# Two layers of a hybrid decoder on one core: meetings with fewer waits for stores, a tile ahead of its meeting, and one sum fewer per selection pass

## What is computed

```python
def split_in(h): ...
    (cb, cc, ch, cg, sq, sk, sv, sg, dq, dk, dv, dg, iq, ik, iw) = split_in(h)
def stick_breaking(q, k, v, q_pos, k_pos):
    z = jnp.einsum('bqhd,bkhd->bhqk', q, k).astype(jnp.float32) * HEAD_DIM ** -0.5
    after = lax.cumsum(log_keep, axis=3, reverse=True) - log_keep
    a = jnp.where(causal, jnp.exp(log_beta + after), 0.0)
def dsa_attend(q, qi, wi, q_pos, k, v, ki, k_pos, topk):
    s = jnp.einsum('bqhe,bke->bqhk', qi, ki).astype(jnp.float32)
    score = jnp.einsum('bqhk,bqh->bqk', jax.nn.relu(s), wi.astype(jnp.float32))
    _, idx = lax.top_k(score, topk)
    ...
x <- LayerNorm(alpha * x + out)
```

## Time and profile before

| | |
|---|---|
| median of three runs | 4813.23 us (4813.03 to 4815.8) |
| the profiled execution | 4808.28 us |
| its span | 4806.6 us |
| busy in the span: TensorE, VectorE, ScalarE, GpSimd | 94%, 71%, 39%, 31% |
| first layer: index from / sample index / projection | 6.9 / 370.7 / 434.8 us |
| stick-breaking / sparse attention / sample attention / output | 1254.2 / 1583.3 / 1916.2 / 2161 us |
| second layer: the same seven | 2409.3 / 2773.4 / 2837.5 / 3655.3 / 3982.7 / 4313.9 / 4558 us |

### The profile page before, as it was taken

How to read it: one execution, slowest core, us unless ns; L and a number is a source line. 1 busy time by engine, 2 the same in 40 slices (tenths; PEclk the granted TensorE clock), 3 DMA queues, 4 the chain that set the end, 5 groups by cost and what they waited for, 6 DMA issues and landing times. The chain is left out here.

```text
span 4806.6 us, 71089 instructions
## 1 busy us (share of the span) xinstructions
PE 4534.3 (94%) x25390; PEld 2600.6 (54%) x25390; DVE 3414.9 (71%) x5595; ACT 1871.0 (39%) x2666; POOL 1466.2 (31%) x1393
## 2 busy tenths in 40 slices
PE   8988999999899998999989889999999999989899
PEld 6433545744566666564464235457445666665643
DVE  2785999999688654554527859999996986545545
ACT  3553223321366665330035532233213666753300
POOL 4310146300163794110032101463001537941100
PEclk9999999999999999999999999999999999999999
DMA  2102111211321003885211021112113210038832
GB/s 78 31 18 69 53 23 34 76 52 51 108 80 59 23 28 94 276 268 165 97 47 30 18 69 53 23 34 78 51 55 103 81 57 23 28 107 276 266 131 89
DMA packets 343729, 396.43 MB, mean 82 GB/s; under 512 B 100311, under 2 KB 264242, under 8 KB 340050
## 3 DMA queue, kind: packets, MB, share of 16 engines
q1 hardware_dynamic: 318034, 375.10, 25.0%
q10 hardware_dynamic: 25344, 16.79, 1.3%
HBM read 297.71 MB, written 94.14 MB: 82 GB/s over the span
## 5 line engine op out<-in xcount | busy, mean ns | idle before, releaser
L1027 DVE TENSOR_SCALAR_CACHE_REDUCE arena<-arena 128x1536 uint8<-128x1536 f32 (+12 forms) x832 | 1118.6, 1407 | 0.0
L870 PE MATMUL banks<-arena 128*128 128x512 f32 x2176 | 937.4, 592 | 0.0
L870 PEld LDWEIGHTS banks<-arena 128*128 128x128 f32 x2176 | 409.9, 189 | 520.4 <-issue 520.4
L873 PE MATMUL banks<-arena 128*128 128x384 f32 (+1 forms) x2048 | 621.7, 460 | 2.4 <-POOLq L142 2.4
L1343 DVE TENSOR_TENSOR_SCAN arena<-arena 128x129 f32<-128x129 f32 (+3 forms) x480 | 538.7, 1174 | 81.3 <-ACT arena L1254 67.1
L1543 POOL TENSOR_SCALAR arena<-arena 128x128 f32<-128x128 f32 (+14 forms) x180 | 513.2, 2864 | 46.8 <-DVE arena L1569 43.9
L873 PEld LDWEIGHTS banks<-arena 128*128 128x128 f32 x2048 | 380.9, 189 | 208.2 <-issue 2.8
L453 DVE SCALAR_TENSOR_TENSOR arena<-arena 128x512 f32<-128x512 f32 (+3 forms) x532 | 404.2, 760 | 122.8 <-ACT arena L421 73.9
L2074 PE MATMUL banks<-arena 128*128 128x512 f32 x1024 | 444.8, 597 | 15.7 <-DMA arena<-in_w_out 15.7
L1558 DVE CUSTOM_DVE_ANT_0 arena<-banks,arena 128x512 f32<-128x512 f32 (+3 forms) x480 | 269.7, 607 | 233.0 <-PE banks L1469 232.4
L421 ACT ACTIVATE arena<-banks 128x1024 f32<-128x1024 f32 (+3 forms) x304 | 278.4, 920 | 247.0 <-PE banks L360 140.9
(11 more groups left out here) (201 smaller groups left out, 6080.1 us busy)
## 6 DMA issues: line engine op xcount, KB each, us to landing
arena<-in_cache_sb_kv SPq DMA_DIRECT2D x256, 384.0 KB, 4.2
arena<-in_cache_dsa_kv SPq DMA_DIRECT2D x144, 128.0 KB, 4.2
arena<-in_x_prompt SPq DMA_DIRECT2D x32, 512.0 KB, 4.3
arena<-mixT SPq DMA_DIRECT2D x32, 512.0 KB, 4.1
arena<-xs SPq DMA_DIRECT2D x32, 512.0 KB, 4.4
arena<-in_cache_dsa_kv ACTq DMA_DIRECT2D x112, 128.0 KB, 4.6
arena<-in_w_in SPq DMA_DIRECT2D x8, 1536.0 KB, 7.5
out<-arena SPq DMA_DIRECT2D x64, 192.0 KB, 1.9
```

The costliest lines, as they stand in the source:

```text
L870: m = nc.tensor.matmul(bank[i % 4][:, :], W2[c % 2][:, k, j * P:(j + 1) * P], xT[:, k, t * FREE:(t + 1) * FREE], start=(k == 0), stop=(k = ...
L873: m = nc.tensor.matmul(bank[i % 4][:, 0:WD[name]], xT[:, k, t * P:(t + 1) * P], W2[c % 2][:, k, 0:WD[name]], start=(k == 0), stop=(k == KC ...
L1027: nc.vector.tensor_scalar(dummy[j % 2][:, 0:v.shape[-1]], v, thr[:, t:t + 1], 0.0, ALU.is_ge, ALU.add, accum_out=history[:, k, t:t + 1]).t ...
```

## The change

It has four parts. (A) The meeting between the first layer's output and the second layer's index: SyncE no longer waits there for the stores of x; TensorE and ScalarE arrive, take tile 0 of x (still in SBUF) through its transposes and index columns, and meet ahead of step 1. Each transfer of a later x tile waits for the store of its own rows, and VectorE and GpSimd wait for all stores at the start of their index programs. (B) The waits for stores at the ends of stages 4 and 5 move to the start of the next stages: to SyncE, VectorE (at job 12 of sparse attention) and GpSimd, and at stage 6 to SyncE and ScalarE. (C) Selection: only the sample rows are compared without a sum; tile 15 is counted in the same instruction as the other tiles; a pass begins with the sample rows, then tiles 14 and 15; ScalarE makes one sum a pass and not two, at slots of its own. (D) Sample index: SyncE's sixteen page loads of round 2 (e = 0) are issued at the end of the index stage, ahead of the meeting, and ScalarE issues all its sixteen loads in round 1, four behind each relu.

```diff
--- before.py
+++ after.py
@@ -279,6 +279,8 @@
                     sp.wait_ge(s_ff[1], at(s_ff[1], l * NF + XFILL[t - 2] + 1))
+                    if l:
+                        sp.wait_ge(s_ost[t % 2], at(s_ost[t % 2], 16 * ((l - 1) * OUSES[t % 2] + t // 2 + 1)))
@@ -300,6 +302,7 @@
                 sample_keys_load(sp, l, 1, e)
+            sample_keys_load(sp, l, 2, 0)
@@ -338,9 +341,14 @@
+            for c in range(2):
+                if l:
+                    pe.wait_ge(s_ore[c], at(s_ore[c], l * (NT + 1)))
...
             for s in range(NT + 3):
+                if l and s == 1:
+                    meet(pe, l * NBAR)
@@ -400,9 +408,13 @@
+            if l:
+                act.wait_ge(s_omix, at(s_omix, 7 * l))
...
             for s in range(NT + 3):
+                if l and s == 1:
+                    meet(act, l * NBAR)
@@ -434,6 +446,8 @@
                 later_vector(dve)
+            else:
+                rows_stored(dve, l)
@@ -472,6 +486,8 @@
+            if l:
+                rows_stored(pool, l)
@@ -543,7 +559,6 @@
             new_rows(1)
-            sample_keys_load(sp, l, 2, 0)
@@ -633,9 +648,8 @@
                     relu(g, c)
-                    if c and g in (1, 2):
-                        j = 2 * (c - 1) + 8 * (g - 1)
-                        sample_keys_load(act, l, 3, 1, j, j + 2)
+                    if c and g == 1:
+                        sample_keys_load(act, l, 3, 1, 4 * (c - 1), 4 * c)
@@ -994,24 +1008,20 @@
         NSTEP = 4 + 2 * NBIT
-        s_sum = sem("comparisons_summed", 2)
-        SUMMED = (NT - 1, NT)
-        COUNTED = [t for t in SELTILES if t not in SUMMED]
-        PASS = [SUMMED[0]] + COUNTED[9:] + [SUMMED[1]] + COUNTED[:9]
+        s_sum = sem("comparisons_summed")
+        PASS = [NT, NT - 2, NT - 1] + [t for t in SELTILES if t < NT - 2]
...
             PCOLS.append(PCOLS[-1] + (FREE if kind == "F" else WD[name] if t < NT else WD[name] // 2))
-        SUM_SLOTS = [40 * k + x for k in range(NPASS) for x in (9, 27)]
+        SUM_SLOTS = [40 * k + 19 for k in range(NPASS)]
...
-            return sum(1 for x in SUM_SLOTS if x * PCOLS[NPU] < 1536 * PCOLS[i])
-        def sum_scalar(act, l, m):
-            k, t = m // 2, SUMMED[m % 2]
-            act.wait_ge(s_cnt, at(s_cnt, l * NCOUNT + k * NSEL + PASS.index(t) + 1))
-            w = scores(t).shape[-1]
-            nc.scalar.activation(compared[:, 0:w], compared[:, 0:w], ACT.Copy, accum_out=history[:, k, t:t + 1]).then_inc(s_sum, 1)
+            return sum(1 for x in SUM_SLOTS if x * PCOLS[NPU] < 1500 * PCOLS[i])
+        def sum_scalar(act, l, k):
+            act.wait_ge(s_cnt, at(s_cnt, l * NCOUNT + k * NSEL + 1))
+            nc.scalar.activation(compared[:, 0:NKEY], compared[:, 0:NKEY], ACT.Copy, accum_out=history[:, k, NT:NT + 1]).then_inc(s_sum, 1)
@@ -1019,15 +1029,15 @@
                     v = scores(t)
-                    if t in SUMMED:
-                        dve.wait_ge(s_sum, at(s_sum, 2 * (l * NPASS + k) + SUMMED.index(t)))
+                    if t == NT:
+                        dve.wait_ge(s_sum, at(s_sum, l * NPASS + k))
...
                 dve.wait_ge(s_cnt, at(s_cnt, n + NSEL * (k + 1)))
-                dve.wait_ge(s_sum, at(s_sum, 2 * (l * NPASS + k + 1)))
+                dve.wait_ge(s_sum, at(s_sum, l * NPASS + k + 1))
@@ -1174,9 +1184,6 @@
                     load_sparse_queries(sp, l, 1)
-            for u in range(2):
-                sp.wait_ge(s_bys[u], at(s_bys[u], 96 * (l + 1)))
-            sp.wait_ge(s_bs, at(s_bs, 16 * HDSA * NB * (l + 1)))
@@ -1434,7 +1441,20 @@
+        def stick_rows_stored(eng, l):
+            for u in range(2):
+                eng.wait_ge(s_bys[u], at(s_bys[u], 96 * (l + 1)))
+        def sample_bias_stored(eng, l):
+            eng.wait_ge(s_bs, at(s_bs, 16 * HDSA * NB * (l + 1)))
+        def sparse_rows_stored(eng, l):
+            for u in range(2):
+                eng.wait_ge(s_dys[u], at(s_dys[u], 32 * (l + 1)))
         def sparse_sync(sp, l):
+            stick_rows_stored(sp, l)
+            sample_bias_stored(sp, l)
@@ -1450,8 +1470,6 @@
                     load_new_rows(sp, l)
-            for u in range(2):
-                sp.wait_ge(s_dys[u], at(s_dys[u], 32 * (l + 1)))
@@ -1535,6 +1553,7 @@
             J0 = l * NDJ
+            sample_bias_stored(pool, l)
@@ -1545,6 +1564,8 @@
             for e in range(NDJ + 1):
+                if e == 12:
+                    stick_rows_stored(dve, l)
@@ -1694,6 +1715,7 @@
             U0, V0 = l * NAU, l * NAV
+            sparse_rows_stored(sp, l)
@@ -1853,6 +1875,7 @@
             U0, V0, C0 = l * NAU, l * NAV, 4 * NB * l
+            sparse_rows_stored(act, l)
@@ -1980,6 +2003,10 @@
+        def rows_stored(eng, layers):
+            for v in range(2):
+                eng.wait_ge(s_ost[v], at(s_ost[v], 16 * OUSES[v] * layers))
@@ -2029,9 +2056,9 @@
                 sp.dma_start(y_rows(l, t), oo[t % 2][0:rows_of(t), :]).then_inc(s_ost[t % 2], 16)
-            for v in range(2):
-                sp.wait_ge(s_ost[v], at(s_ost[v], 16 * OUSES[v] * (l + 1)))
-            sp.wait_ge(s_osc, at(s_osc, 16 * (l + 1)))
+            if l == DEPTH - 1:
+                rows_stored(sp, DEPTH)
+                sp.wait_ge(s_osc, at(s_osc, 16 * DEPTH))
@@ -2169,7 +2196,10 @@
             for l in range(DEPTH):
-                barrier(pe, l * NBAR)
+                if l:
+                    arrive(pe)
+                else:
+                    barrier(pe, 0)
@@ -2189,7 +2219,10 @@
             for l in range(DEPTH):
-                barrier(act, l * NBAR)
+                if l:
+                    arrive(act)
+                else:
+                    barrier(act, 0)
...
```

## The result

| | before | changed |
|---|---|---|
| median, us | 4807.91 (7 runs) | 4785.56 (7 runs) |
| range of the runs | 4804.11 to 4815.8 | 4774.19 to 4793.91 |
| ratio of changed to before | | 0.995 [0.994, 0.996] |
| span of the profiled execution | 4806.6 | 4785.6 |

The change takes 0.5% off: 24 us by the ratio, 19 to 29 by its interval; 31.6 were forecast.

What follows compares the result with a forecast made beforehand. In the projection TensorE is busy 806.77 of 814 us, so only its stalls counted there; elsewhere its waits at meetings and in the sample index. 3.7 + 6.2 + 7.1 + 10.6 + 4.0 = 31.6 off 4813.2: 4781.6 us, range 4769 to 4800.

Steps and rivals of the forecast that it cites:

- the first rival: Sample index gives nothing: later meeting certain, the wait for keys replaced by another wait; 4792.2 us, chance 0.11.
- Sparse attention's meeting: Meeting before sparse attention: without SyncE's wait for its last store TensorE starts 1.9 us earlier, twice, 3.7 us.
- Sample attention's meeting: Meeting before sample attention: TensorE's scores begin 0.8 us behind the last sparse store's landing, 3.1 a layer, 6.2 us.
- The rival that it is given back: Sample attention gives its 6.2 us back by reaching each page earlier and waiting longer; 4787.8 us, chance 0.06.
- Between the layers: Meeting before the second layer: TensorE and ScalarE start the first tile ahead of it; first product 7.1 us earlier.
- about 6.5 us behind ScalarE's last statistic: Sign of being right: where TensorE's first product of the second layer would stand after ScalarE's last statistic before it.
- The sample index: Meeting 4.1 and 7.5 us later, but waits for keys go and round 3's clock rises; gains 6.5 and 4.1, 10.6.
- The clock as a rival: Sample index: rounds 2 and 3 could run at 1.2 GHz, losing round 3's 1.9 us in both layers; 4785.4, chance 0.08.
- The projection: TensorE's 3.86 us stall shrinks by about one ScalarE sum, 2.0 us a layer, 4.0 us in all.
- VectorE's slack: VectorE's wait at the projection's end: 33.8 us before, 17 to 22 left after the change, at no cost for TensorE.
- the other signs: TensorE busy over 809 of 814 us; no key wait over 1; attention-meeting SyncE waits at most 0.5; sample index some 52.5.

Runs made afterwards that it cites:

- the shifted kernel: Nine SyncE loads ahead, ScalarE's two at a time, plus 20 ScalarE register loads ending the first projection; 4771.68 us, ratio 0.9925 to the kernel before.

## Why the prediction was right or wrong

The sign, the range (4769 to 4800) and the order of size were right: 31.6 forecast, about 24 measured, 21.0 between the traces. That the time came within 4.0 us of the forecast (4785.56 against 4781.6) is partly luck: the forecast was taken off 4813.23, the median of three runs, and the median of seven is 4807.91. Against that the forecast would be 4776.3 and the first rival, a sample index that gives nothing, 4786.9; the rival is the nearer one, and its mechanism is the one that the traces show. Term by term:

- **Sparse attention's meeting**, 3.7: right. 2.2 and 1.6 by the stretches, and the wait of 2.71 became 0.97, twice. (The estimate of 2.6 us that the prediction took from the Trainium skill is stated there for transfers of GpSimd's path. This store is on SyncE's queue, and the measured 2.3 decides.)
- **Sample attention's meeting**, 6.2: right. 3.5 and 3.2 up to the scores, 0.8 behind the landing as worked out. The rival that it is given back holds in part for one layer of the first trace (−1.4 behind the scores, of 3.2 won); on the mean of the traces it does not, which they lean to and do not prove.
- **Between the layers**, 7.1: by the run without the part 4 to 5. The mechanism was right to 0.5 us (10.7 became 4.1 to the first product), but the products took 1.4 longer at a slower clock, which was not in the sum. (The sign "about 6.5 us behind ScalarE's last statistic" does not follow from the prediction's own times: 2405.6 less 2402.03 is 3.6, and 4.1 was measured. 6.6 is what was saved.)
- **The sample index**, 10.6: wrong, and the step that failed. From mask to projection it gave 0.3 and −2.3. The late meeting was foreseen (4.1 and 7.5; 4.9 and 7.3 measured), the vanished wait for keys too, and round 3 gained 2.3 us where 1.9 were taken for its clock. Of 11.6 between meeting and projection in the second layer 5.0 were left (64.0 to 59.0), less than the delay. The 6.6 that are missing: the longer wait at the meeting put round 0 on a slow clock (0.74, 2.2 us longer). And the stretch of round 2 with the wait for keys behind it, which was to lose 9.3, lost 5.2 (22.7 to 17.5): ScalarE's load was taken at 0.71 each, from a row of two, and took 0.88 to 0.96 in bursts of four; TensorE stood 2.8 to 3.0 us behind these bursts three times, once in round 2 itself, where the prediction had them only stand in for the wait for new rows; and round 2 began at a clock of 0.52. Round 1, which was to end 0.4 earlier, ended 0.3 later. Taking the sixteen loads as one thing to move was the error: nine fitted into what SyncE had free ahead of the mask (322.38 to 370 less 32 loads, and 2727.81 to 2773 less 32: 13 and 10 us, 12 and 9 loads), and that division could have been read from the rows.
- **The clock as a rival**: half true. Round 2 ran at 0.52 to begin with, as the rival says, but round 3 at 1.00. The granted clock was 0.50 at the end of TensorE's wait of 8.16 us and until 2763.8; then 1.00, through the wait of 2.98; then 0.50 again from 2784.3 to 2797.9, through the waits of 2.82 and 2.78. By the Trainium skill ("TensorE: Matmul & The Clock Gate", "HAM oscillation — how this bites in real kernels") waits for transfers between bursts of matmuls slow the engine before every burst. The trace agrees where TensorE had stood still just before, though for SyncE and ScalarE and not for a transfer; round 3, which had no wait ahead of it, did not pay.
- **The projection**, 4.0: 4.9 less 2.4. In the first layer the sum's removal did what was said. In the second the row of the stall was right, but its cause there was another sum, late because VectorE was late, because a store had landed late. VectorE's slack was 16.2 and 15.2, just below the 17 to 22 forecast. The prices behind it were right: the form with a running sum took 2.34 us at 2048 for the 2.35 forecast (32 passes are then 32 us, not 33), and the waits for sums in the first layer fell to 0.5. Where the late store struck, the one buffer for comparisons passed the delay on to VectorE.

Of the other signs, TensorE was busy for 810.3 of 814 us in the first projection (809 were asked for), and no wait for keys was left. The wait for SyncE at the attention meetings was to be under 0.5 and is 0.97, and the sample index was to take 52.5 us and takes 59.

The sum of the parts in the traces is smaller than the whole. A gave 4 to 5, B 10.5 up to the scores, C 2.5 and D −2.0, about 15.5 of 21.0; most of the rest is the clock of the second layer's index stage, shown beside part A, which no part is shown to have changed.

## What to carry to other kernels

When work is moved ahead of a meeting, count what the moving queue has free before the meeting's present last arrival, and move only that much. Here, with ScalarE's loads two at a time, nine loads of sixteen gave 10.0 and 10.6 us in the two layers from mask to projection (some 6 less in two of the ten stages seen), and all sixteen 6.6 and 3.6; all sixteen with ScalarE's bursts of four gave 0.3 and −2.3. Issues on a computing engine should be spread so that none of its short steps waits behind a burst; price a burst by its length and not by the pair that the trace shows. And where one buffer couples two engines through a sum, one late transfer can shift the second engine for the rest of the stage: here by 8 us.

The version with nine loads ahead is the best that was run: 4759 to 4763 us, ratio 0.9896 and 0.9903 to the kernel before, 0.4 to 0.5% below the changed one; with the small store moved its second projection is 5 us shorter, with no difference in the total that these runs could tell.

## What was not expected of the hardware

A 256 KB store whose data had all moved within 2.5 us released its waiter only after 10.4 us, at about the time at which the 1 KB store of 4-byte rows issued right behind it landed (10.3 us). That small store takes about as long everywhere (11.0 in the second layer of the kernel before); what differs is whether the large one ahead of it is released without it. It was held in the second layer of all nine traces of kernels with part C and that order (ScalarE's wait 21.2 to 22.3). It was not held in their first layers, where the projection took 814.5 us but for the shifted kernel's, nor in either layer of the two without part C (wait 14.7, release 2.3 us behind the issue).

The DMA records show a 16 KB instruction fetch beside it. The eleven traces with the small store at its old place hold 44 such pairs of stores. In the nine late ones a fetch started between 0.1 us before and 0.4 us after the issue of the large store (3030.04 beside an issue at 3029.97 in the changed kernel), and the issue of the small one took 0.86 to 1.52 us. In the second layers of the two kernels without part C the fetch started 0.6 and 1.0 us before the large store; in the other 33 pairs there was none within 3 us. None of these 35 was late, and the small store's issue took 0.43. With the small store moved the fetch was there too, 0.1 and 0.2 us before the large store, and nothing was late (13.99 and 13.85). So the late release was seen only with both together, and that the small store is needed is shown by the two runs that moved it. For the fetch there is a coincidence in time, in nine of nine cases, and no experiment: whose it is was not found (it did not move with ScalarE's program), and a run that moves SyncE's or VectorE's fetches alone was not made.
